# A two-layer hybrid trunk: the RWKV scan's first operands loaded earlier, and the head's first block projected in two halves

## The reference

```python
def _hybrid_layer(x, ...):
    h = _rmsnorm(x, norm_g)
    proj = h @ w_in                       # 1024 x 3972, columns split among four mixers
    y_fox  = _fox_attention(...)          # forgetting attention, blocks of 128
    y_rwkv = _rwkv7_time_mix(r_pre, ...)  # token shift, decay, delta-rule scan over time
    y_swa  = _swa_attention(...)          # sliding window with sinks
    y_conv = _short_conv(cb, cc, cx, conv_w)
    mixed = concat([y_* * silu(gate_*)])
    return x + mixed @ w_out

def step(state, inp):                     # the RWKV scan, per token and head
    sa = einsum("bhvk,bhk->bhv", state, -kk_t)
    state = state * w_t + sa[..., None] * (kk_t * a_t) + v_t[..., None] * k_t
    return state, einsum("bhvk,bhk->bhv", state, r_t)
```

## Time and profile before

| | us |
|---|---|
| median of three runs | 3008.51 |
| the three runs | 3010.51, 3005.77, 3008.51 |
| profiled execution, its own time | 3006.9 |
| its span, first to last instruction | 3005.1 |
| mean granted TensorE clock | 0.978 |

### The profile page before, as it was taken

The page is one execution under the profiler, slowest core; times in us unless marked ns, Lnnn a source line. Parts: engine busy times, 40 slices in busy tenths (PEclk is TensorE's granted clock), DMA queues, the critical chain, the costliest instruction groups (busy, mean ns, idle before and its releaser), DMA issues. The chain is left out here.

```text
span 3005.1 us, 67947 instructions
## 1 busy us (share of the span) xinstructions
PE 2850.2 (95%) x26454; PEld 2116.1 (70%) x26454; DVE 1601.3 (53%) x2372; ACT 1103.4 (37%) x2226; POOL 1071.2 (36%) x996
## 2 busy tenths in 40 slices
PE   7999989999999799989979999899999997998999
PEld 6878867777777554467768788677777775544777
DVE  5877732223222387767458777322333323877774
ACT  5124433333333234633151244333333332346331
POOL 5111122455555423632151111224555554246321
PEclk9999999999999899999989999999999998999999
DMA  6445443444444351266354455333444444412663
GB/s 206 156 139 174 156 113 97 117 120 126 129 128 131 118 140 40 86 200 206 116 192 157 141 171 164 110 93 114 130 128 132 128 130 123 134 41 85 203 206 113
DMA packets 443461, 405.17 MB, mean 135 GB/s; under 512 B 128808, under 2 KB 367784, under 8 KB 442888
## 3 DMA queue, kind: packets, MB, share of 16 engines
q1 hardware_dynamic: 378088, 368.07, 40.4%
q10 hardware_dynamic: 65056, 32.77, 4.1%
HBM read 261.47 MB, written 139.17 MB: 133 GB/s over the span
## 5 line engine op out<-in xcount | busy, mean ns | idle before, releaser
L147 PE MATMUL ch_acc<-h_hi,ch_w_hi 128*128 128x512 f32 x1968 | 786.8, 400 | 9.3 <-PEq L144 8.2
L153 PE MATMUL ch_acc<-h_hi,ch_w_lo 128*128 128x512 f32 x1968 | 793.6, 403 | 0.0
L151 PE MATMUL ch_acc<-h_lo,ch_w_hi 128*128 128x512 f32 x1968 | 789.4, 401 | 0.0
L151 PEld LDWEIGHTS ch_acc<-h_lo,ch_w_hi 128*128 128x128 f32 x1968 | 369.8, 188 | 87.8 <-issue 11.1
L147 PEld LDWEIGHTS ch_acc<-h_hi,ch_w_hi 128*128 128x128 f32 x1968 | 369.9, 188 | 84.9 <-issue 10.5
L153 PEld LDWEIGHTS ch_acc<-h_hi,ch_w_lo 128*128 128x128 f32 x1968 | 369.6, 188 | 79.5 <-issue 0.3
L115 POOL TENSOR_TENSOR ch_w_lo<-ch_raw,ch_w_hi 128x1024 fp32r<-128x1024 f32 x60 | 154.6, 2576 | 579.4 <-POOLq L114 579.4
L164 ACT COPY ch_stage<-ch_acc 128x512 f32<-128x512 f32 x232 | 136.0, 586 | 438.8 <-ACTq L163 438.7
L1910 ACT ACTIVATE fx_prob<-fx_ST 128x512 f32<-128x512 f32 (+3 forms) x320 | 154.1, 531 | 188.7 <-PE fx_ST L1757 96.0
L2165 PE MATMUL so_acc<-ea_wo_hi,so_m_hi 128*128 128x512 f32 x512 | 209.2, 409 | 7.1 <-POOL so_m_lo L2100 3.7
L962 POOL TENSOR_SCALAR rs_qx<-rs_qx,ch_room 128x256 f32<-128x256 f32 x112 | 103.8, 927 | 288.3 <-ACT rs_qr L1255 271.0
(11 more groups left out here) (296 smaller groups left out, 4826.0 us busy)
## 6 DMA issues: line engine op xcount, KB each, us to landing
projT<-ch_stage SPq DMA_DIRECT2D x248, 256.0 KB, 2.4
pj_xb<-x SPq DMA_DIRECT2D x64, 512.0 KB, 4.1
ch_raw<-w_in ACTq DMA_DIRECT2D x62, 512.0 KB, 5.4
so_stage<-x SPq DMA_DIRECT2D x64, 256.0 KB, 3.1
ch_room<-projT SPq DMA_DIRECT2D x16, 899.5 KB, 7.6
rs_qx<-projT SPq DMA_DIRECT2D x112, 128.0 KB, 3.3
ch_room<-rw SPq DMA_DIRECT2D x192, 64.0 KB, 2.5
rs_cs<-rope SPq DMA_DIRECT2D x48, 256.0 KB, 3.5
```

What stands on the lines that cost most here:

```text
L147: ins = M(acc, self.w_hi[q][:, k, 0:m], self.h_hi[:, k, cols], start=(k == 0), stop=False)
L151: M(acc, self.w_hi[q][:, k, 0:m], self.h_lo[:, k, cols], start=False, stop=False)
L153: ins = M(acc, self.w_lo[q][:, k, 0:m], self.h_hi[:, k, cols], start=False, stop=(k == KC - 1))
```

## The change

Four parts, named here A to D; the diff follows, cut to its core.

A. **Operands of the scan.** `room` is laid out so that masks, gains, `cr0` and the `pend` factors lie in `pre[0]` and `bt`, `kt`, `nat` in `pre[1]`. SyncE loads masks and gains in unit 6 and the first tile's operands in unit 7, part ahead of the unit's stores. `left` is raised as soon as VectorE has finished the last unit, ahead of its stores; a second semaphore `kept` follows when the stores have landed, and only VectorE waits for it, in the middle of tile 0. What must outlive the preparation shares one buffer, `held`. TensorE no longer waits for `i_ok`, GpSimd no longer for `left`.

B. **ScalarE in the preparation.** In every unit `act_split` moves from behind the last exponential to a place ahead of the low-rank tanh.

C. **The head's first block** is done in two halves of 256 columns, each hi·hi, then `w_lo`, then `h_lo`, with the transposes of tiles 3, 4 and 5 between them; the transposes of tiles 6 and 7 now follow 8 and 16 matmuls of the second row. The first `w_lo` is made by GpSimd, ahead of everything else there.

D. **ScalarE in the head.** The raw weights' load goes first, and the order is: factor 0, 1, split, factor 2, rounded 0, 1, factor 3, rounded 2, factor 4, rounded 3, factor 5.

```diff
+    def pe_first(self, pe, q, rdy):
+        M, acc, half = self.nc.tensor.matmul, self.acc[q], TB // 2
...
+        for i in range(2):
+            cols = slice(i * half, (i + 1) * half)
+            for part, (w, h) in enumerate(((self.w_hi, self.h_hi), (self.w_lo, self.h_hi), (self.w_hi, self.h_lo))):
+                rdy(i, part)
+                if i == 0 and part == 1:
+                    pe.wait_ge(self.w_rdy[q], 1)
...
-    def load_scan(self, sp):
+    def load_masks(self, sp):
         sp.dma_start(self.ident, self.consts[:, 0:128]).then_inc(self.m_in, 16)
-        self.load_chunks(sp, 0, self.cr0, 0)
-        self.load_chunks(sp, 0, self.cr0, 2)
-        self.load_tokens(sp, 0)
...
+    def load_gains(self, sp):
...
# phase_project, ScalarE
+            J.act_load(act, R_PRE)
             factor(0)
-            J.act_load(act, R_PRE)
-            for t in range(1, BT):
-                factor(t)
+            factor(1)
+            J.act_split(act, 0)
+            factor(2)
             rounded(0)
+            rounded(1)
+            factor(3)
+            rounded(2)
             factor(BT)
-            rounded(1)
-            J.act_split(act, 0)
-            rounded(2)
             rounded(3)
             factor(BT + 1)
# GpSimd
+            J.pool_weights(pool, 0)
             for t in range(NT):
# TensorE
-            for t in range(BT):
+            for t in range(3):
                 turn(t)
...
+            def rdy(i, part):
                 if part == 0:
-                    pe.wait_ge(s["hi_rdy"], BT)
-                if part == 1:
-                    pe.wait_ge(s["lo_rdy"], BT - 1)
-                    pe.wait_ge(s["lo3_rdy"], 1)
+                    pe.wait_ge(s["hi_rdy"], 2 * i + 2)
+                if part == 2:
+                    pe.wait_ge(s["lo_rdy"], 2 + i)
+                    if i == 1:
+                        pe.wait_ge(s["lo3_rdy"], 1)
...
+            for n, t in ((2 * KC, 3), (KC, BT), (2 * KC, BT + 1), (KC, None)):
+                for _ in range(n):
+                    next(begin)
+                if t is not None:
+                    turn(t)
             for i in range(3):
                 for _ in range(KC):
-                    next(begin)
-                if i > 0:
-                    turn(BT + i)
-            for _ in range(KC):
-                next(tile[1])
-            turn(BT + 3)
-            for _ in range(2 * KC):
-                next(tile[1])
+                    next(tile[1])
+                if i < 2:
+                    turn(BT + 2 + i)
# VectorE (scaled is L477, gained L485)
+                if t < NT and t != 2:
+                    scaled(t)
                 if 0 < t <= NT:
+                    gained(t - 1)
+                if t == 2:
+                    scaled(t)
                 if t == BT:
-                    J.pool_weights(v, 0, 128, V)
# phase_rwkv_prep, SyncE
+                last = i == NU - 1
...
+                if last:
+                    X.load_chunks(sp, 0, X.cr0, 0)
...
                 put(i, 4, xs[:, 4:6, :], s["v_st"])
+                if last:
+                    sp.wait_ge(pre_free[q], 1)
+                    X.load_chunks(sp, 0, X.cr0, 2)
                 J.sp_store(sp, row, 0)
+                if last:
+                    X.load_tokens(sp, 0)
                 J.sp_store(sp, row, 1)
-                if i == NU - 1:
-                    for q in two:
-                        sp.wait_ge(pre_free[q], 1)
-                    X.load_scan(sp)
+                if i == NU - 2:
+                    sp.wait_ge(pre_free[q], 1)
+                    X.load_masks(sp)
+                if last:
+                    sp.wait_ge(s["v_st"], 16)
                 sp.wait_ge(s["out_rdy"], 1)
                 sp.sem_inc(s["out_rdy"], -1)
+                if last:
+                    sp.sem_inc(X.left, 1)
...
                 J.sp_store(sp, row, 2)
+                if i == NU - 2:
+                    X.load_gains(sp)
                 J.sp_store(sp, row, 3)
...
             sp.wait_ge(s["out_st"], 80)
-            sp.sem_inc(X.left, 1)
+            sp.sem_inc(X.kept, 1)
# phase_rwkv_prep, ScalarE
                 evac(i, "th")
+                J.act_split(act, q)
                 act.wait_ge(s["lora_rdy"], 1)
...
                 A(nrm, nrm, ACT.Exp, scale=-0.5).then_inc(s["nrm_rdy"], 1)
-                J.act_split(act, q)
                 evac(i, "ssk")
                 evac(i, "bs")
# phase_rwkv_scan
-            pool.wait_ge(X.left, 1)
...
                     pe.wait_ge(X.left, 1)
                     pe.wait_ge(s["c_in"], 96)
-                    pe.wait_ge(s["i_ok"], 1)
...
+                if t == 0:
+                    v.wait_ge(X.kept, 1)
+                    V.memset(S[:], 0.0)
+                    for e_ in two:
+                        V.tensor_copy(cr[e_][:, :, 2, :], eye...)
+                    v.drain().then_inc(s["s2_d"], 1)
```

More of the change, by code:

```diff
@@ L116, in pool_weights @@
         pool.drain().then_inc(self.raw_free, 1)
-    def pe_first(self, pe, q, parts_rdy):
-        M, acc, cols = self.nc.tensor.matmul, self.acc[q], slice(0, TB)
+    def pe_first(self, pe, q, rdy):
+        M, acc, half = self.nc.tensor.matmul, self.acc[q], TB // 2
         pe.wait_ge(self.acc_free[q], 1)
         pe.sem_inc(self.acc_free[q], -1)
-        for part, (w, h) in enumerate(((self.w_hi, self.h_hi), (self.w_hi, self.h_lo), (self.w_lo, self.h_hi))):
-            parts_rdy(part)
-            if part == 2:
-                pe.wait_ge(self.w_rdy[q], 1)
-                pe.sem_inc(self.w_rdy[q], -1)
-            for k in range(KC):
-                ins = M(acc[:], w[q][:, k, :], h[:, k, cols], start=(part == 0 and k == 0), stop=(part == 2 and k == KC - 1))
-                if part == 2 and k == KC - 1:
-                    ins.then_inc(self.acc_rdy[q], 1)
-                yield
+        for i in range(2):
[4 more added lines that the diff above has]
+                    pe.wait_ge(self.w_rdy[q], 1)
+                    pe.sem_inc(self.w_rdy[q], -1)
+                for k in range(KC):
+                    ins = M(acc[:, cols], w[q][:, k, :], h[:, k, cols], start=(part == 0 and k == 0), stop=(part == 2 and k == KC - 1))
+                    if i == 1 and part == 2 and k == KC - 1:
+                        ins.then_inc(self.acc_rdy[q], 1)
+                    yield
     def pe_tile(self, pe, q, m=128, par=None, frees=0, first=0):
@@ L180 @@
     PB = 256
+    HELD = 2624
     def __init__(self, P, nc, l, projT, par, lora, consts, masks, rw, pend):
@@ L187, in __init__ @@
         self.p_in, self.c_in = [P.sem(f"p_in{q}") for q in self.two], P.sem("pc_in")
-        self.left, self.i_in, self.m_in, self.n_in = P.sem("left"), [P.sem(f"i_in{e}") for e in self.two], P.sem("m_in"), P.sem("n_in")
+        self.left, self.kept, self.pend_st, self.i_in, self.m_in, self.n_in = P.sem("left"), P.sem("kept"), P.sem("pend_st"), [P.sem(f"i_in{e}") for e in self.two], P.sem("m_in"), P.sem("n_in")
         self.at = 0
@@ L266, in phase_project @@
         NX, NG, BT = 4, 3, TB // 128
-        xb = [P.sb(f"xb{q}", [128, DM]) for q in range(NX)]
+        xb = [X.held[:, q * DM:(q + 1) * DM] for q in range(2)] + [P.sb(f"xb{q}", [128, DM])[:] for q in range(2, NX)]
         gw = P.sb("gw", [128, NH, DM])
@@ L778, in phase_rwkv_scan, with held @@
         p8 = p2
[L779 to L780 removed]
+        px, q4, wz = (P.sb(n, [128, NH, 2, 64]) for n in ("px", "q4", "wz"))
+        gm = px
+        at = 0
+        def held(*shape):
+            nonlocal at
+            n = int(np.prod(shape))
+            at += n
+            v = X.held[:, at - n:at]
+            return v if len(shape) == 1 else v.rearrange(f"p ({' '.join('abc'[:len(shape)])}) -> p {' '.join('abc'[:len(shape)])}", **dict(zip("abc", shape)))
+        S, yst = held(NH, 64), held(2, 128)
         yt, yc, yq = p4, x1, yy
         ym, yv = P.sb("ym", [128, NH, 1]), P.sb("yv", [128, NH, 1])
[L783 removed]
         bk = P.ps("bk", [128, 6, 512])
@@ L786, in phase_rwkv_scan @@
         bones = X.bones
-        qx = [P.sb(f"qx{e}", [128, UB]) for e in range(3)]
-        qp = [P.sb(f"qp{e}", [128, UB]) for e in two]
-        cs = P.sb("cs", [128, 2, UB])
+        qx = [held(UB) for e in range(3)]
+        qp = [held(UB) for e in two]
+        cs = held(2, UB)
         qh = [P.sb(f"qh{e}", [128, UB], F32R) for e in two]
@@ L1166, in _ @@
             v.wait_ge(X.left, 1)
-            V.memset(S[:], 0.0)
             V.memset(zi[:, 0, :], 0.0)
             v.wait_ge(s["c_in"], 96)
-            for e in two:
-                V.tensor_copy(cr[e][:, :, 2, :], eye.rearrange("p (o t) -> p o t", o=1).to_broadcast([128, NH, 64]))
             V.memset(eps[:], EPS)
```

77 lines of the change are left out of this document (39 added, 38 removed).

## The result

The changed kernel is slower: 3027.61 us against 3009.51 us in the same measurement (medians of four runs each), ratio 1.0057, 95% interval 1.0036 to 1.0079. Forecast were 2997 us and a range up to 3012; both the sign and the range are missed. Measured once more beside the first experiments, the change gave 3030.56 us against 3010.54 (ratio 1.0063, 1.0048 to 1.0079). The profiled execution took 3019.69 us, span 3017.9, the shortest of its four runs; before it was 3006.9 and 3005.1. So the profiles stand 12.8 us apart and the medians 18.1.

What follows compares the result with a forecast made beforehand. TensorE was taken as the bound nearly everywhere. The terms -26.7 + 6.2 + 9 = -11.5 against the profiled 3006.9 gave 2995.4, and 1.6 for the median of the runs made it 2997 us; range 2981 to 3012.

Steps and rivals of the forecast that it cites:

- A, -26.7: Transition to the scan: 22.9 us of TensorE waits go, and 3.8 us come from a clock that stays up.
- B, +6.2: Preparation: the split ahead of the tanh adds 10.5 us of waits over 14 units, less 4.3 in unit 1.
- -4.3 for unit 1: Preparation, unit 1: two waits of 1.10 and 1.04 us go, -2.1 per layer, -4.3 in all.
- take 5.4 us to land: Preparation: raw weights issued at the unit's start land 5.4 us later, the median of 3.9 to 7.4.
- a new wait of 0.75 us: Preparation, block 3: TensorE waits 0.75 us for its bank in each of 14 units, +10.5 us.
- rival 2: Preparation: the split ahead of the tanh makes the kernel slower, up to 3025 us at the longest landing; chance 0.09.
- the exemption weighed in the prediction: Preparation, L635: if single-input VectorE work escapes the port lock, the wait is near 0.1 us per unit, B about -3.
- C and D, +9: Head, both layers: TensorE starts earlier, but the chain feeding it is later, +9 us; bounds 0 and +8 per layer.
- split and two roundings come ahead of factor 3 ...: 13.4: Head, ScalarE: split and two roundings, about 1.0 us each, move factor 3 from 10.38 to 13.4.
- TensorE can start on 256 tokens: Head, first block: TensorE starts after two roundings instead of four, near 14 us instead of 19.
- I take 4.5 of the 5.2 us: Head, second block: tile 7's transpose moves from 34.1 to 39.3, of which 4.5 us count as lateness.
- Rival 3: Head: it costs twice as much, by its clock, giving 3006 us, no change; chance 0.16.

Runs made afterwards that it cites:

- run with the prefetch: Parts A and B, each next unit's raw weights loaded behind the last exponential, one unit ahead; 2977.16 us, ratio 0.9895 to the kernel of before.
- run with the later load: Parts A and D, raw weights loaded behind factor 0 as before and the split behind rounded 0; 2990.11 us, ratio 0.9942 to the kernel of before.
- the halves alone: Part A plus only C's two 256-column halves, first low weights on VectorE, all orders of before; 2992.43 us, ratio 0.9948 to the kernel of before.
- the turns first: Parts A and C, transposes of tiles 3 and 4 again ahead of the first block, later ones as before; 2999.89 us, ratio 0.9972 to before.
- more instructions: Part A plus 48 idle transposes per layer ahead of the attention; 2990.65 us, ratio 0.9939 to the kernel of before.

## Why the prediction was wrong

**A, -26.7: right.** The transition gives 27.9 us with A alone. The steps that its rows show all stood: no wait, clock 1.00, 2.1 us to the third group, 8.1 us of cover. The clock's share was a little larger than put: tile 0 is 4.7 us shorter over both layers, forecast were 3.8 with a bound of 4.5. By medians the whole kernel gained 31.8. Of the 4 us beyond, 3 come from the kernel of before, whose profiled execution was 3.6 us under its median there, while A's was 0.9 under its own; the rest is in the spread of the stages.

**B, +6.2: the chain was right, one term mis-sized.** Measured +17.9, of which 14.1 in B's own stages and 2.8 in a head that is A's. The -4.3 for unit 1 came (the step from unit 0 to unit 1 fell from 21.44 to 19.26 us, in both layers). The step that failed is "take 5.4 us to land", and with it "a new wait of 0.75 us": the split starts 6.0 us after the issue on average, and a unit grows by 1.32 us (26.2 - 24.88), 14 times, of which 1.03 is the wait itself and the rest stands in the matmuls around it. 0.75 plus the 0.6 of the later split is that number. Two things make the 0.6. In the trace of the full change, which has landings for layer 1 only, every split of units 1 to 7 starts 0.20 us after the landing, which the prediction left out. And the landings there are 5.66 us by the median, against 5.44 for the same units of the kernel before (its trace has landings for 31 of the 62 loads, those of layer 0). Why they come 0.2 us later is open. The median of all loads was thus not the error, since the units' own was the same 5.4; what failed is to stand on a single value where each 0.1 us counts 14 times. The prediction's own rival 2 had 1.5 us at a landing of 6.1, and 9%. The run with the prefetch shows that without the wait for the landing B costs nothing.

The Trainium skill (SBUF — State Buffer, "Who interferes with whom") says that scaling ops can use the shared port pair and that whoever issues first blocks the other. VectorE's 0.43 us scaling took 1.25 beside the subtraction, and the 0.75 us one 2.76, each with the subtraction started first, so the trace agrees; the exemption weighed in the prediction did not apply.

**C and D, +9: wrong, and the largest error.** 35 us in all by medians. The head makes 29 of them in the profile with A, C and D and 19 in that of the full change (both against A's), the scans 5 to 7. Three steps failed.

- "split and two roundings come ahead of factor 3 ...: 13.4". It came at 16.41. The split had waited 2.41 us for a load issued 9.8 us earlier, and tile 1 of x was a microsecond later (factor 1 at 7.69, before 6.74). The prediction did not ask what the load issued at 2.11 shares its queues with. The Trainium skill (DMA: Bandwidth & Descriptors, "Queues, rings and completion order") says that the DMA engines take turns between the queue rows they have work for; the run with the later load fits it in so far as the load then takes at most 5.3 us instead of 9.8; the turns themselves no run shows.
- "TensorE can start on 256 tokens" was costed by its start. That tiles 3 and 4 are transposed behind matmuls which need GpSimd, and that GpSimd's 2.4 us stand in front of every low part and beside a scaling, was left out: C was costed at nothing beyond tile 7, and alone it costs 30.4. In layer 0 the second block stands at 40.15 with A, at 41.38 with the halves alone, at 45.98 with GpSimd's first subtraction and the orders around it, and at 49.19 with the turns: 1.2, 4.6 and 3.2 us. In the full change part of this is hidden by D, and the other way round.
- "I take 4.5 of the 5.2 us". The second block came 8.8 later. Of the 4.3 us too few, 2.0 are the second row (36.64 instead of 34.6, by the two steps above), 1.5 the clock behind the wait of 4.55 us (6.2 us from the second row to tile 7 instead of 4.7), and 0.7 were taken as regained: the second block stands 6.0 us behind the transposes of tile 7 before (34.19 to 40.23) and 6.15 after (42.87 to 49.02). In executions like the one with A, C and D the head takes nearly 5 us more again per layer, most of it by the clock. Rival 3 had named the clock, and the bound was +8 per layer: the head took 8.5 more than before in the profile of the full change and 13.4 in the other.

**What no step had.** The 24 added matmuls per layer "are hidden in the waits" as far as their time goes: in layer 0 the halves alone put the second block 1.2 us later. The 48 matmuls of 256 columns start 0.12 us apart at full clock and 0.21 at half, so the 109 ns weighed in the prediction were a little low. The count of the added ones moves TensorE's stalls to other places, and the scans of the full change are 6.3 us longer; with A alone, adding as many records in idle time makes them 5.9 us longer.

**The sum.** Measured by medians -31.8 + 17.9 + 35.0, against -26.7 + 6.2 + 9. Of the 30.6 us between 2997 and the median, 26 are those of C and D (the head and the scan's stalls), 12 are B's, and A gave 5 back; these add up to 32.6, and the 2 us between are within the measurement.

## What to carry to other kernels

Where a wait hangs on a transfer and is paid in every unit, carry the spread of its landings through the sum and not their median: 0.6 us more than the median cost 8 us here. Where a load is moved, ask what it will share the queues with. A load issued one unit earlier cost nothing in the preparation and turned B's loss into none. An operation that feeds others (here a transpose) must not be put behind work that waits for the slowest engine: "starts earlier" is worth nothing where the end hangs on the feed. And a change with a clean gain should be timed without its companions: here A gained 32 us, and B and the pair of C and D lost 53.

## What the runs showed of the hardware

In the scans TensorE stands still for 0.9 to 1.9 us at certain places of its own instruction count, where it waits for no semaphore. In thirteen kernels with three different counts every such stall of over 0.9 us fell on a record number (of all its records, waits included) that leaves 193 when divided by 256; not every such number stalls, and which ones are felt changes when instructions are added anywhere ahead. The five kernels with 0.2% more TensorE records (54538 against 54442) had scans 5 to 15 us longer than A's. What lies behind the 256 no run shows.

Whether the clock falls behind a short idleness differs between executions and kernels. The stall at record 36545 was followed by 8 us at a mean granted clock of 0.57 with the halves alone (a stall of 1.64 us) and with the turns first (1.66), and by an unbroken 1.00 with more instructions (1.67). In the head a gap of 3.12 us ahead of the second block was followed by 0.50 in one profile, and one of 3.27 us by 1.00 in another, at the same code.
